# Attention softmax on one Trainium2 core: turned-map copies ahead of the share diagonals on ScalarE, one reciprocal per pair

## What is computed

```python
# group A, 6 heads, window + bias + all context keys
p = jax.nn.softmax(jnp.concatenate([s_lat, s_ctx], axis=-1), axis=-1)
# group B, 4 heads, two maps per head
p = jax.nn.softmax(s, axis=-1)
pd = (p[:, :, 0] - lam * p[:, :, 1])
# group C, 6 query heads on 2 key/value heads
p = jax.nn.softmax(s, axis=-1)
```

## Time and profile before

| | before |
|---|---|
| median of 3 runs | 4273.56 us |
| the profiled execution, its own time | 4269.68 us |
| its span | 4267.5 us |
| TensorE busy | 2875.5 us (67%) |
| VectorE busy | 2803.6 us (66%) |
| ScalarE busy | 1466.1 us (34%) |
| GpSimd busy | 1284.7 us (30%) |
| DMA, mean over the span | 354 GB/s |
| attention loop, layer 0 | about 362 to 670 us |
| attention loop, layer 1 | about 2454 to 2706 us |

### The profile page before, as it was taken

How to read it: one execution, slowest core, us unless ns; L and a number is a source line. 1 busy time by engine, 2 the same in 40 slices (tenths; PEclk the granted TensorE clock), 3 DMA queues, 4 the chain that set the end, 5 groups by cost and what they waited for, 6 DMA issues and landing times.

```text
span 4267.5 us, 47616 instructions
## 1 busy us (share of the span) xinstructions
PE 2875.5 (67%) x16592; PEld 1294.0 (30%) x16592; DVE 2803.6 (66%) x5874; ACT 1466.1 (34%) x4706; POOL 1284.7 (30%) x1306
## 2 busy tenths in 40 slices
PE   7896887866566556655657978885555555555655
PEld 4555664422221122311112656442111111111111
DVE  1378777787647846665674799678765675774554
ACT  2115674322233322222233378432222222222222
POOL 1002222123333333343333222122333333333332
PEclk9998898978877788778777989997777767777877
DMA  9638886679999999999997777566999999999997
GB/s 350 224 137 334 349 325 255 231 277 406 413 409 403 409 414 407 415 417 420 412 405 314 266 265 278 199 257 261 413 417 419 418 409 419 418 408 413 418 418 318
DMA packets 230192, 1508.71 MB, mean 354 GB/s; under 512 B 25408, under 2 KB 29504, under 8 KB 64960
## 3 DMA queue, kind: packets, MB, share of 16 engines
q0 software_dynamic: 185504, 1353.53, 79.2%
q1 hardware_dynamic: 44448, 152.14, 9.6%
HBM read 1501.38 MB, written 4.19 MB: 353 GB/s over the span
## 4 chain that ended last, share of the span: by engine, by line
DMA 41%; PE 26%; DVE 20%; issue 6%; ACT 5%; POOL 2%; SPq 0%; ACTq 0%; DVEq 0%; POOLq 0%
DMA work<-expert_dram,work 40%; PE psum L938 10%; DVE work L1837 5%; PE psum L970 4%; DVE work L1883 4%; PE psum L783 3%; PE psum L876 3%; DVE work L1891 2%; POOL work L2101 2%; ACT work L1311 1%; PE psum L853 1%; PE psum L787 1%; PE psum L837 1%; DVE stat L1625 1%; ACT work L1302 1%
## 5 line engine op out<-in xcount | busy, mean ns | idle before, releaser
L938 PE MATMUL psum<-work 64*64 64x512 f32 x8192 | 1426.3, 826 | 1103.8 <-ACT work L1311 1103.7
L1837 DVE SCALAR_TENSOR_TENSOR work<-work,psum 128x1024 f32<-128x1024 f32 x1024 | 1247.2, 1219 | 987.6 <-DMA work<-expert_dram,work 980.1
L2101 POOL DMA_INDIRECT work<-expert_dram,work x1024 | 977.1, 954 | 1735.4 <-PE psum L938 1603.1
L938 PEld LDWEIGHTS psum<-work 64*64 64x64 f32 x8192 | 327.8, 168 | 2142.9 <-ACT work L1311 1877.8
L1302 ACT ACTIVATE work<-work 128x2 f32<-128x2 f32 x512 | 104.1, 203 | 1908.5 <-DVE work L1837 1908.5
L2083 POOL DMA_INDIRECT work<-expert_dram,work x256 | 278.3, 1087 | 1142.1 <-DVE work L1883 872.9
L1891 DVE SCALAR_TENSOR_TENSOR work<-work 128x1024 f32<-128x1024 f32 x256 | 312.9, 1223 | 101.7 <-DMA work<-expert_dram,work 101.1
L1311 ACT ACTIVATE work<-const,work 128x128 f32<-128x128 f32 x1024 | 347.4, 386 | 0.0
L1883 DVE SCALAR_TENSOR_TENSOR work<-work 128x1024 f32<-128x1024 f32 x254 | 327.7, 1290 | 15.6 <-ACT work L1342 15.1
L890 PE MATMUL psum<-work,ring 128*128 128x512 f32 x512 | 233.6, 611 | 30.4 <-ACT work L1155 30.4
L1305 ACT ACTIVATE work<-work 128x1 f32<-128x1 f32 x1024 | 245.7, 287 | 16.8
(11 more groups left out here) (207 smaller groups left out, 2937.7 us busy)
## 6 DMA issues: line engine op xcount, KB each, us to landing
ring<-w_mod_dram SPq DMA_DIRECT2D x85, 512.0 KB
ring<-w_in_dram SPq DMA_DIRECT2D x63, 512.0 KB
ring<-w_query_dram SPq DMA_DIRECT2D x60, 512.0 KB
work<-expert_dram,work POOLq DMA_INDIRECT x1280, 8.7
ring<-w_out_dram SPq DMA_DIRECT2D x30, 512.0 KB
work<-w_in_dram SPq DMA_DIRECT2D x17, 512.0 KB, 5.5
work<-w_mod_dram SPq DMA_DIRECT2D x11, 512.0 KB, 5.1
work<-rpb_dram POOLq DMA_DIRECT2D x2, 2688.0 KB, 17.8
```

The source lines that it names most:

```text
L938: last = pe.matmul(out[to:to + HP, cols_], diag[tok, n % NDIAG, tok], rows[(SLOTS * t + s) % NBUF][tok, D + 512 * half:D + 512 * half + 51 ...
L1837: dve.scalar_tensor_tensor(u, u, 1.0, pair[0], ALU.mult, ALU.mult, accum_out=act_in[:, s:s + 1]).then_inc(dot_done, 1)
L2101: pool.indirect_dma_start(rows[m % NBUF], None, a[f"expert{l}"], bass.IndirectOffsetOnAxis(expert[:, t % 2, s:s + 1], 0)).then_inc(row_in[ ...
```

## The change

On ScalarE the two blocks of a step change places: the copies of pair k-1 come first, the diagonals of pair k behind them. On VectorE the two one-column reciprocals of a pair become one of two columns, behind a wait for both exponentials; `inv_set` counts pairs instead of maps. In B the product with -lambda stays. Nothing else is touched: TensorE's stream and the expert stages are as they were.

```diff
@@ ScalarE, attention, behind the exponentials @@
-                    for n in (2 * k, 2 * k + 1) if k < NPAIR else ():
-                        act.wait_ge(inv_set, NMAP * l + n + 1)
-                        if k >= 2:
-                            act.wait_ge(tr_done, NITEM * l + MAPS[n - 4]["item"] + 1)
-                        act.activation(shares_[:, n % 4, :], con("ident"), ACT.Copy,
-                                       scale=stat[:, 2, n % NPROB:n % NPROB + 1]).then_inc(share_set, 1)
                     turned = pair_items(k - 1)
                     for i in turned:
...
                         act.activation(probT[:, it["unit"] % 2, it["hh"], 0:w], flat[:, turn_at(i):turn_at(i) + w],
                                        ACT.Copy).then_inc(pt_done, 1)
+                    for n in (2 * k, 2 * k + 1) if k < NPAIR else ():
+                        act.wait_ge(inv_set, NPAIR * l + k + 1)
+                        if k >= 2:
+                            act.wait_ge(tr_done, NITEM * l + MAPS[n - 4]["item"] + 1)
+                        act.activation(shares_[:, n % 4, :], con("ident"), ACT.Copy,
+                                       scale=stat[:, 2, n % NPROB:n % NPROB + 1]).then_inc(share_set, 1)
@@ VectorE, attention, behind the first context slot @@
-                    for n in (2 * k, 2 * k + 1):
-                        m, s = MAPS[n], n % NPROB
-                        dve.wait_ge(exp_done, NMAP * l + n + 1)
-                        last = dve.reciprocal(stat[:, 2, s:s + 1], stat[:, 1, s:s + 1])
-                        if m["kind"] == "B" and m["c"] == 1:
-                            link(last)
-                            last = dve.tensor_scalar(stat[:, 2, s:s + 1], stat[:, 2, s:s + 1], nlam[:, l:l + 1], None,
-                                                     ALU.mult)
-                        last.then_inc(inv_set, 1)
+                    s = 2 * k % NPROB
+                    dve.wait_ge(exp_done, NMAP * l + 2 * k + 2)
+                    last = dve.reciprocal(stat[:, 2, s:s + 2], stat[:, 1, s:s + 2])
+                    if MAPS[2 * k]["kind"] == "B":
+                        link(last)
+                        last = dve.tensor_scalar(stat[:, 2, s + 1:s + 2], stat[:, 2, s + 1:s + 2], nlam[:, l:l + 1], None,
+                                                 ALU.mult)
+                    last.then_inc(inv_set, 1)
```

## The result

The changed kernel took 4253.07 us (median of 6 runs, 4247.56 to 4259.24) where the kernel before took 4273.1 us (6 runs, 4265.3 to 4278.52). The ratio is 0.9947, 95% interval 0.9933 to 0.9961: faster, by 17 to 29 us, about half a per cent. A second set of 6 runs gave 4251.37 us against 4276.09 and 0.9948 [0.993, 0.9966]. The forecast was 4252.7 us. The profiled execution of the changed kernel took 4259.24 us, span 4257.1 us; those of the kernel before took 4269.68 and, in a repeat, 4268.73 us.

A forecast was written before the change was run, and what follows sets the result against it. Layer 1 was taken as nearly VectorE's alone, layer 0 as shared by VectorE, TensorE and DMA. Terms 10.8 + 4.1 + 4 + 2 = 20.9 us off 4269.68 gave 4248.8, plus 3.9 for the median: 4252.7 us; range 4237 to 4268.5.

The forecast's parts named there:

- Copies ahead of diagonals: Both attention loops: values products start earlier, so VectorE's waits shrink, 10.8 us for scores and 4.1 us for exponentials.
- the term of 10.8 us: Both attention loops: half of the 21.6 us of VectorE's score waits left after setting 10 us aside; ends 0 and 21.6.
- three kinds of waits: VectorE in layers 0 and 1: scores 21.9 and 9.7 us, exponentials 8.9 and 5.6, rows 16.7 and 4.1.
- the rival in which memory takes it: Attention loops: VectorE then waits for rows and TensorE for ring blocks, leaving 6 us of gain, 4267.6 us; chance 0.20.
- a sign of being wrong: Layer 0: VectorE's row waits grow by what its score waits lose.
- The ends of the loops: Last steps of both loops: values products' waits for copies, 3.25 and 1.84 us, go; 4 us taken, ends 3 and 5.1.
- One reciprocal: VectorE, 80 pairs: each second reciprocal costs 0.05 us, 4.0 us in all, half on the chain: 2 us, ends 0 and 4.0.
- I cost it at nothing: VectorE's added wait of the reciprocal for the pair's second exponential: 0 us, or 0.35 us if the cover were gone.
- the rule that removes the full 0.16 us: VectorE: by the skill's DRAIN text each removed reciprocal saves 0.16 us, 12.8 us in all; the forecast doubted it.
- The clock: Rival: fewer idle gaps raise TensorE's granted clock in layer 0, 9 us beyond the forecast, 4243 us; chance 0.17.
- Slower, by late diagonals: Rival, wide pairs of B and C: diagonals late behind copies awaiting their turning, 13.5 us lost, 4283 us; chance 0.07.

The follow-up runs named there:

- light loads: Kernel before and changed kernel, each loading only the first 64 KB of each 512 KB block of layer 1's modulation weights: layer 0's loop 295.7 and 280.7 us.

## Why the prediction was right, and where it wasn't

**The total.** 4252.7 us was forecast, 4253.07 and 4251.37 us were measured, and the range held both. The working says less: by stages the change is worth 15.5 us, not 20.9. The agreement with the timed median owes 5 to 9 us to a difference that no stage of the profiles shows. That part is luck.

**Copies ahead of diagonals: right in mechanism, its parts mis-sized.** For the loops without their ends I had 10.8 + 4.1 = 14.9 us. The loops lost 15.5 us, of which the stretch from the last scores to the output projection holds 1.7 us in layer 0 (20.9 to 19.2) and about 1 us in layer 1 (16.2 and 15.8 before, 14.5, 15.5 and 14.6 after). That leaves 12.7 us. The step that failed is the term of 10.8 us, and with it the sign that VectorE's waits for scores "should drop by ten us or more": they fell by 7.0 us (3.1 and 3.9), and by 2.0 us only if line 1625 alone is counted, as in the earlier trace rows. The forecast had left out 9.7 us of waits in line 1624 when it called its three kinds of waits nearly all of VectorE's idle time; in layer 0 they are 47.5 of 62.1 us. The waits for exponentials fell by 4.5 us, where 4.1 was taken.

**The memory: right in kind, but in both layers.** I took half of the waits for scores "because two thirds of it are in layer 0, where a faster VectorE meets its rows". Rows took back 4.4 us in layer 0 and 3.3 us in layer 1, half or more of what the other waits lost in either. So the rival in which memory takes it was true by half, and of layer 1 too, where it had been argued away. In layer 0 the row waits grew by more than the score waits lost, which the forecast had named as a sign of being wrong. I had about 12 us for layer 0 and 9 for layer 1; measured were 7.7 and 7.8. With light loads the same edit gave 15.0 us in layer 0, so the full loads hold the gain down there; the way in which they do is open, as said above.

**The ends of the loops: 4 us taken, 2.8 measured.** The step that failed is "both go to the end of the stage". In layer 0 the wait of 3.25 us became 1.39 us, as the two copies that now come first take 1.30 us themselves:

```profile
654.09 1.30 ACT L1239 ACTIVATE work<-psum 128x640 f32<-128x640 f32 x2
...
655.44 2.40 PE L837 MATMUL psum<-work 128*64 128x128 f32 x20 [1.39 <-ACT work L1239]
```

In layer 1 the wait of 1.84 us did vanish, but in this execution the last turning then waited 1.00 us for the values copy:

```profile
2682.83 1.31 PE L837 MATMUL psum<-work 128*64 128x128 f32 x20
...
2692.65 0.71 PE L853 MATMUL psum<-work 128*128 128x128 f32 x4 [1.00 <-ACT work L1230]
```

**One reciprocal: no gain found.** I took 2 us, between 0 and 4.0. VectorE's busy time did fall by it, by 2.6 and 2.4 us a loop, but the step "I cost it at nothing" left something out: in B the merged signal makes the first diagonal wait for the product with -lambda as well. I had looked only at the wait for the second exponential. The wait for the product is seen in the timeline; what it costs is not shown. Alone the merge came out 3.5 us slower in the timed runs, with an interval from no change to 13 us slower. On top of the order the profiles make it 2 to 4 us slower in layer 0 (311.2 against 308.8 with two reciprocals everywhere and 307.4 with two in B), no different in layer 1, and the timed runs make it a few us faster, all within their spread. The doubt about the rule that removes the full 0.16 us held: 80 instructions fewer took 5.0 us off VectorE's busy time, 0.06 us each. The Trainium skill, VectorE: DVE Perf Modes, says in the same section, "The DRAIN you can't avoid", that a next operation that is not held starts earlier. The trace agrees with that: two reciprocals in a row take 0.21 us and one alone 0.16 us.

**The clock: didn't move with full loads.** 0.85 and 0.93 before and after, with 44 us less waiting in front of the values products. Much of the idle time moved to the next group: turnings wait 17.8 + 14.9 us in layer 0 for diagonals and the values copy, where they waited 10.5 + 6.4, and TensorE idles 69.4 us of that loop where it idled 75.2 (length minus busy in the windows). It rose only with the light loads, 0.88 and 0.91.

**Slower, by late diagonals: small.** Copies wait for turnings 12 and 10 times in the changed kernel, where it was 8 and 11: more in layer 0, as forecast, and not in layer 1. Turnings now do wait for diagonals: 17.8 us in layer 0, of which 12.0 us is the first turning of the loop, where the kernel before waited 10.5 us too. The 5.8 us that are left are in a loop that got shorter all the same.

## What to carry to other kernels

Put what is ready first in an in-order stream: an engine that idles for a result should do, ahead of that wait, whatever needs nothing from it. Price such a change by the idle time of the engine that bounds the stage, not by the waits that vanish, of which there were 81 us here (36.7 of diagonals, 44.5 of values products) for 15.5 us of time; and expect part of it to come back as waits for loads, as half of VectorE's did here. A stage that shares the memory with large loads may give less still: 7.7 us here against 15.0 with light loads. Before two signals are merged into one, list what each of the waiting instructions really reads: a merge that saves an instruction can hold back one that didn't need the slower half. And before a difference of a few us is read from one profile, profile the same kernel again: loops of 250 to 320 us moved by up to 5 us here with nothing changed in them.

## What the runs showed that I had not expected

Loading only an eighth of each of 44 blocks of 512 KB made layer 0's loop 23 us shorter in one execution with no other edit (318.9 to 295.7 us), although the loads are asked for ahead through a ring of four: these loads cost more than the change gave. And the profiled executions of the kernel before lie 3 to 7 us under the medians of its timed runs (4269.68 and 4268.73 against 4273.1 to 4276.09), while those of the changed kernel lie 4 to 8 us above theirs (4259.24, 4256.66 and 4259.11 against 4253.07 and 4251.37). One profile of each would have shown half of the timed difference. The cause stays open. It may be the draw alone: the timed runs of the changed kernel by themselves reach from 4243.29 to 4259.24 us, and there are two and three profiles.
